# A gather of 32,768 expert rows: two tables with one indirect DMA each, against one table with the up row beside the down row

## The reference

```
query = (ht @ w_query).reshape(t, 8, 2, 128)
sub_scores = einsum('thpd,hpkd->thpk', query, sub_keys)
half_vals, half_idx = top_k(sub_scores, 16)
...                                          # 16 x 16 candidates, top 16 of them
experts = i1 * 128 + i2
gates = softmax(top_vals)
u = expert_down[experts]
act = gelu(einsum('td,thkd->thk', x, u)) * gates
vv = expert_up[experts]
out = einsum('thk,thkd->td', act, vv)
```

## Time and profile before

| what | value |
|---|---|
| time, median of 3 runs | 1837.53 us (1836.64 to 1842.37) |
| span of the profiled execution, first to last instruction | 1792.6 us |
| median less span | 44.9 us |
| first gather issued, last gather issued | 342.6 us, 1051.2 us |
| first matmul of the stage after the gathers | 1074.4 us |
| busy: PE, DVE, POOL, ACT | 78%, 59%, 39%, 26% of the span |
| bytes by the gathers | 268.47 MB |

### The profile page before, as it was taken

How to read it: one execution, slowest core, us unless ns; L and a number is a source line. 1 busy time by engine, 2 the same in 40 slices (tenths; PEclk the granted TensorE clock), 3 DMA queues, 4 the chain that set the end, 5 groups by cost and what they waited for, 6 DMA issues and landing times.

```text
span 1792.6 us, 16903 instructions
## 1 busy us (share of the span) xinstructions
PE 1399.6 (78%) x6336; PEld 971.5 (54%) x6336; DVE 1062.6 (59%) x1736; ACT 469.3 (26%) x708; POOL 694.8 (39%) x643
## 2 busy tenths in 40 slices
PE   1698858756766767787777779856999979879997
PEld 1696547722322222232222238745999877669996
DVE  3546854999987744644444435466544557664545
ACT  0332343211111111211111123232443335324331
POOL 1205600277878777777777730000111105102110
PEclk9999978978999999899999999967999989989999
DMA  8744552599999999999999963204455524335550
GB/s 261 257 162 150 205 164 95 202 348 358 358 336 348 362 379 403 405 387 409 410 407 407 410 248 138 98 1 164 157 198 188 188 97 141 109 132 182 189 188 24
DMA packets 160066, 433.17 MB, mean 242 GB/s; under 512 B 17120, under 2 KB 17376, under 8 KB 159856
## 3 DMA queue, kind: packets, MB, share of 16 engines
q0 software_dynamic: 73728, 268.47, 39.0%
q1 hardware_dynamic: 79344, 159.89, 25.6%
q10 hardware_dynamic: 6912, 3.73, 0.8%
HBM read 431.00 MB, written 1.05 MB: 241 GB/s over the span
## 4 chain that ended last, share of the span: by engine, by line
PE 42%; DVE 24%; POOL 14%; DMA 8%; issue 6%; ACT 4%; ACTq 1%; DVEq 0%
PE PS L43 41%; POOL PR L37 7%; POOL SCR L37 6%; DMA SCR<-in_expert_up,EI 5%; DVE PR L76 4%; DMA PR<-in_expert_down,EI 3%; DVE WL L73 2%; DVE LNV L61 2%; DVE LNV L49 2%; DVE GV L73 2%; ACT WH L22 2%; PE PS L82 2%; DVE X L61 2%; DVE LNV L46 1%; ACTq L34 1%
## 5 line engine op out<-in xcount | busy, mean ns | idle before, releaser
L43 PE MATMUL PS<-SCR,BIG 128*128 128x512 f32 x1024 | 507.9, 632 | 188.0 <-DMA SCR<-in_expert_up,EI 98.3
L43 PEld LDWEIGHTS PS<-SCR,BIG 128*128 128x128 f32 x1024 | 187.6, 198 | 507.1 <-issue 371.7
L76 DVE CUSTOM_DVE_ANT_0 PR<-PR,Y 128x1024 f32<-128x1024 f32 x256 | 312.3, 1222 | 223.5 <-DMA PR<-in_expert_down,EI 223.2
L73 DVE TENSOR_TENSOR WL<-W,WH 128x4096 fp32r<-128x4096 f32 x60 | 266.4, 4440 | 211.3 <-ACT WH L22 210.4
L37 POOL DMA_INDIRECT PR<-in_expert_down,EI x256 | 268.3, 1048 | 197.6 <-DVE ST L58 115.2
L37 POOL DMA_INDIRECT SCR<-in_expert_up,EI x256 | 278.5, 1088 | 80.4 <-issue 60.4
L43 PE MATMUL PS<-XH,WH 128*128 128x256 f32 x960 | 277.2, 289 | 15.1 <-POOL XL L73 9.5
L43 PE MATMUL PS<-XH,WL 128*128 128x256 f32 x960 | 272.8, 284 | 0.0
L43 PE MATMUL PS<-XL,WH 128*128 128x256 f32 x960 | 272.7, 284 | 0.0
L22 ACT ACTIVATE WH<-W 128x4096 fp32r<-128x4096 f32 x60 | 217.6, 3626 | 117.5 <-PE PS L43 104.3
L73 POOL TENSOR_TENSOR AL<-Y,AH 128x512 fp32r<-128x512 f32 x32 | 41.8, 1307 | 489.2 <-DVE AH L64 489.2
(11 more groups left out here) (166 smaller groups left out, 1467.3 us busy)
## 6 DMA issues: line engine op xcount, KB each, us to landing
W<-in_ffn_w SPq DMA_DIRECT2D x32, 2048.0 KB, 8.8
W<-in_w_ada SPq DMA_DIRECT2D x12, 2048.0 KB, 8.3
W<-in_w_in SPq DMA_DIRECT2D x6, 2048.0 KB, 7.9
W<-in_hy_w_in SPq DMA_DIRECT2D x6, 2048.0 KB, 8.1
W<-in_gla_w_in SPq DMA_DIRECT2D x6, 2048.0 KB, 7.8
W<-in_w_query SPq DMA_DIRECT2D x4, 2048.0 KB, 8.2
W<-in_w_out SPq DMA_DIRECT2D x2, 2048.0 KB, 8.4
PR<-in_expert_down,EI POOLq DMA_INDIRECT x256, 6.6
```

What stands on the lines that cost most here:

```text
L43: return lambda e: e.matmul(*a, **k)
L73: return lambda e: e.tensor_tensor(*a, **k)
L76: return lambda e: e.tensor_tensor_reduce(*a, **k)
```

## The change

The host lays the down row and the up row of an expert side by side in one table `experts` of 2048 columns. One indirect DMA fetches both for a slot, 8 KB for each partition, into one of 8 buffers `EBUF` that together take the place of `PR0` and `SCR`. The dot reads the first half, the matmuls the second. A buffer is free after the matmuls. Gates are computed for 2 slots at a time, `up` follows two slots behind the dot where it was 12, the steps of `later` come three after each dot from the first slot on, and the first split after the gathers is recorded behind the loop, with the subtraction on POOL in place of DVE.

```diff
-        PR0 = sb("PR0", [128, 8192])
-        SCR = sb("SCR", [128, 8192])
+        EB = sb("EB", [128, 16384])
+        SCR = EB[:, 8192:16384]
...
-        def split(later=False):
+        def split(later=False, by=dve):
...
-                td = dve(lambda e: e.tensor_tensor(WL[p][:, :, :], W[:, s, :, :], WH[p][:, :, :].bitcast(F32), ALU.subtract),
-                         ta, tw, *free)
+                td = by(lambda e: e.tensor_tensor(WL[p][:, :, :], W[:, s, :, :], WH[p][:, :, :].bitcast(F32), ALU.subtract),
+                        ta, tw, *free)
...
+        EBUF = [EB[:, i * 2048:(i + 1) * 2048] for i in range(NB)]
+        es = [Slot(sem(f"s_e{i}")) for i in range(NB)]
+        e_free = [pair_free[i // 4] for i in range(NB)]
...
-        LAG, GRP, EARLY = 12, 8, 8
+        GRP, LAG = 2, 3
...
+        def gather(s):
             t, j = s // 128, s % 128
+            i = s % NB
+            landed[s] = pool.dma(lambda e: e.indirect_dma_start(
+                out=EBUF[i], out_offset=None, in_=A["experts"][:, :],
+                in_offset=bass.IndirectOffsetOnAxis(ap=EI[:, t, j:j + 1], axis=0)), es[i], *e_free[i], t_e[t, j // 32])
+
+        def dot(s):
+            u = EBUF[s % NB][:, 0:1024]
+            return dve(lambda e: e.tensor_tensor_reduce(
+                out=u, in0=u, in1=Y[:, s // 128, :], scale=1.0, scalar=0.0,
+                op0=ALU.mult, op1=ALU.add, accum_out=dots[:, s:s + 1]), landed[s], ordered=False)
...
-            up_tok[s] = gather(UB[i], A["expert_up"], s, us[i], u_free[i])
...
-            pe.wait(tg, up_tok[s], *bank_free[4 + 2 * t], *bank_free[5 + 2 * t])
-            u = UB[s % NB]
+            pe.wait(tg, landed[s], *bank_free[4 + 2 * t], *bank_free[5 + 2 * t])
+            u = EBUF[s % NB]
...
-            u_free[s % NB] = (tk,)
+            e_free[s % NB] = (tk,)
...
-        for s in range(EARLY, total + LAG + 1):
+        for s in range(total + LAG):
             if s < total:
-                down(s)
-                for _ in range((4 if s < 40 else 3) if s < 112 else len(later)):
+                gather(s)
+                td = dot(s)
+                if s % GRP == GRP - 1:
+                    ta = gelu(s, td)
+                for _ in range(3 if s < 112 else len(later)):
...
-            while nu < total and nu <= s - LAG and nu in gated and n < 2:
+            while nu < total and nu <= s - LAG + 1 and nu in gated:
...
+                if nu == total - 4:
+                    pair_free[0] = (tk,)
         assert nu == total
+        split(by=pool)
         t_xt = (t_xt0, finish(1, tk))
...
+    give("experts", np.concatenate([inputs["expert_down"][0], inputs["expert_up"][0]], axis=1))
```

More of the change, by code:

```diff
@@ L1118, in build, with gelu, gate @@
         dg_free = [q_free[1] for _ in range(NDG)]
-        LAG, GRP, EARLY = 12, 8, 8
+        GRP, LAG = 2, 3
         total = 256
-        up_tok = {}
-        gated = {}
-        def gather(dst, table, s, slot, free):
+        landed, gated = {}, {}
+        def gather(s):
             t, j = s // 128, s % 128
[L1126 to L1130, removed]
             i = s % NB
[L1132 to L1138, removed]
+            landed[s] = pool.dma(lambda e: e.indirect_dma_start(
[6 more added lines that the diff above has]
+                op0=ALU.mult, op1=ALU.add, accum_out=dots[:, s:s + 1]), landed[s], ordered=False)
+        def gelu(s, td):
             g = slice(s - GRP + 1, s + 1)
-            ta = act(lambda e: e.activation(acts[:, g], dots[:, g], ACT.Gelu), dve.last)
+            return act(lambda e: e.activation(acts[:, g], dots[:, g], ACT.Gelu), td)
+        def gate(s, ta):
+            g = slice(s - GRP + 1, s + 1)
             td = dve(lambda e: e.tensor_tensor(
@@ L1148, in up @@
             t, j = s // 128, s % 128
-            i = s % NB
-            up_tok[s] = gather(UB[i], A["expert_up"], s, us[i], u_free[i])
             i = s % NDG
             tg = act(lambda e: e.activation(DG[i], ident, ACT.Copy, scale=acts[:, s:s + 1]), *dg_free[i], gated[s], ordered=False)
-            pe.wait(tg, up_tok[s], *bank_free[4 + 2 * t], *bank_free[5 + 2 * t])
-            u = UB[s % NB]
+            pe.wait(tg, landed[s], *bank_free[4 + 2 * t], *bank_free[5 + 2 * t])
+            u = EBUF[s % NB]
             for n in range(2):
-                make = lambda e: e.matmul(PS[4 + 2 * t + n][:, :], DG[i], u[:, n * 512:(n + 1) * 512],
+                make = lambda e: e.matmul(PS[4 + 2 * t + n][:, :], DG[i], u[:, 1024 + n * 512:1536 + n * 512],
                                           start=(j == 0), stop=(j == 127))
@@ L1186, in finish @@
             return turn_tile(X[:, t, :], t, tx)
-        for s in range(EARLY):
-            down(s)
-            later.pop(0)()
-        for s in range(GRP - 1, EARLY, GRP):
-            gate(s)
         nu = 0
-        for s in range(EARLY, total + LAG + 1):
+        for s in range(total + LAG):
             if s < total:
-                down(s)
-                for _ in range((4 if s < 40 else 3) if s < 112 else len(later)):
+                gather(s)
[3 more added lines that the diff above has]
+                for _ in range(3 if s < 112 else len(later)):
                     if later:
@@ L1208, in build @@
                 if s % GRP == GRP - 1:
[L1209 to L1213, removed]
-            while nu < total and nu <= s - LAG and nu in gated and n < 2:
+                    gate(s, ta)
+            while nu < total and nu <= s - LAG + 1 and nu in gated:
                 tk = up(nu)
                 nu += 1
-                n += 1
                 if nu == 128:
                     t_xt0 = finish(0, tk)
+                if nu == total - 4:
+                    pair_free[0] = (tk,)
         assert nu == total
+        split(by=pool)
         t_xt = (t_xt0, finish(1, tk))
@@ L1638 @@
 _LAYERED = ["w_ada", "b_ada", "g_norm_mix", "w_in", "b_forget", "g_out_fox", "g_out_sb", "w_out", "g_norm_ffn",
-            "w_query", "sub_keys", "expert_down", "expert_up", "hy_w_in_2", "diff_lambda_2", "diff_subln_2",
+            "w_query", "sub_keys", "hy_w_in_2", "diff_lambda_2", "diff_subln_2",
             "hy_w_out_2", "gla_w_in_2", "gla_w_gate_up_2", "gla_b_gate_2", "gla_norm_2", "gla_w_out_2"]
```

## The result

| | before | after |
|---|---|---|
| time, median | 1837.09 us (1836.36 to 1842.37, 4 runs) | 1760.49 us (1758.87 to 1761.89, 4 runs) |
| span of the profiled execution | 1792.6 us | 1758.7 us |
| first matmul of the stage after the gathers | 1074.43 us | 1040.73 us |

The ratio is 0.958 (95% interval 0.956 to 0.960): the change takes 76.6 us off. The forecast was 1788 us with a range of 1766 to 1816, so the sign was right and the size too small by 28 us. Set against the profiled execution of before, the stage that the change touches gained only 33.7 us (1074.43 to 1040.73). The two differences don't fit together, and that is the main question of the experiments.

What follows compares the result with a forecast made beforehand. Two nearly equal limits, POOL's issue and the DMA engines, with DVE right behind POOL in the earlier part. Next stage at 998 + 26.2 = 1024.6, 49.8 us less; span 1792.6 - 49.8 = 1742.8, plus 44.9: 1788 us, range 1766 to 1816.

Steps and rivals of the forecast that it cites:

- plus the 44.9 around it: Last term: time outside the profiled span, median of the runs less the span, added to 1742.8 us to give 1788.
- The sum inside the span: Next stage after the gathers starts at 1024.6 instead of 1074.4 us, 49.8 less, so span 1792.6 becomes 1742.8.
- The rival of 2.56: Gathers: an 8 KB row costs two of 4 KB, slot stays at 2.56 us, 11 us later: 1799; chance 0.20.
- Dot 98: Earlier part of the gathers: DVE sets the pace, 2.57 us for each slot, and this dot ends at 606 us.
- The rival that this part stays at 361 GB/s: Earlier part of the gathers: something other than POOL's issue holds the engines, 2.9 us a slot: 1824 us; chance 0.10.
- the slower rival: Gathers: eight buffers are too few, 2.74 us for each slot, next stage 8 us later: 1845 us; chance 0.08.
- The later part: Gathers from 606 us: 154 slots at 2.49 us, plus 4 for constants and 5 for `finish(0)`; last slot lands at 998.
- T + 26.2: Start of the next stage, counted from T, the last slot's landing at 998 us; includes `finish(1)` waiting for POOL's subtraction.
- The rival without this wait: End of the gathers: `finish(1)` does not wait on POOL, next stage at T + 17.9, time 1780 us; chance 0.15.

Runs made afterwards that it cites:

- the second profile of before: The kernel before, unchanged, profiled and timed again: 1837.6 us, ratio 0.998; span of the profiled run 1832.6 us.
- the run with the slower pace: After, with three and two steps of the choice in turn behind the dots instead of three, constants at slot 120 instead of 112: 1751.28 us, ratio 0.951.

## Why the prediction was wrong, point by point

**The step that failed: "plus the 44.9 around it".** I took the median less the span as a constant that any execution carries. It is 1.8 or 1.9 us in every run that has both. The rest of the 44.9 was time inside the gathers that usual executions of before lose and the profiled one did not. After doesn't lose it, so I carried 43 us into the forecast that were not there. The sum inside the span erred by 16 us the other way, and the two leave the 28. That they cancel in part is luck: with 1.8 in place of 44.9 the same sum gives 1745 us, 16 too few. (998 + 26.2 is 1024.2; the 1024.6 of the sum comes of unrounded terms.)

**What the 44.9 us were.** The earlier trace rows said that POOL's 512 gathers fill the later part with nothing to spare, and I read that as a limit equal to the transfer's. The 18 us of waiting that I read there were mostly the ordinary pause of 0.30; only three waits were longer, 5.6 us in all. An engine without reserve has a second price: each wait is lost for good. In the second profile of before, 37 of the 47 us that the gathers take longer are such waits. The Trainium skill (Perfetto Trace Analysis, "What "DMA-bound" means") names the issuing engine's sequencer as a bound of its own beside the DMA engines, and large descriptors as what matters for both. The runs agree: a gather of 128 rows took POOL the same 0.94 us with rows of 32 bytes, 4 KB and 8 KB, so rows of twice the length halve POOL's work for the same bytes. Whether POOL's time goes by DMAs or by rows is not separated, since every gather here has 128 rows. The runs with memsets show both prices with all DMAs as in after: 2.48 us of POOL for a slot cost 23 us, 2.87 us cost 74. What starts the long waits in usual executions of before stays open. They are 2 to 7 us each where PE frees the buffer and up to 4.8 us where the profile says "remote". The stops of DVE that come with them occur only in profiles with 512 gathers, also where half of them fetch 32 bytes, and not where memsets fill POOL instead; so POOL's lack of reserve explains that the time was lost, and not that the engines stopped. Why the first profiled execution had none of these stops stays open too.

**The transfer.** I took 2.49 us for a slot between 2.36 and 2.56; it is 2.49 (421 GB/s). The rival of 2.56 fell. In the trace's packets a row of 8 KB is one packet and takes 309 to 312 ns at the median; a row of 4 KB took 159 before, so two take 318. At eight rows for each of the 16 engines, 9 ns less for a row is an estimated 0.07 us of a slot, which is the step that I took. The times don't show it by themselves: before, POOL's own 2.56 hid what 4 KB rows can do.

**DVE in the first slots.** Dot 98, the 99th, was forecast to end at 606 us. It ended at 613.75:

```profile
361.93 0.16 DVE L73 TENSOR_TENSOR BIG<-BIG,LNV 128x2 f32<-128x2 f32 x1 [4.08 <-ACT BIG L22]
...
612.53 1.22 DVE L76 CUSTOM_DVE_ANT_0 EB<-EB,Y 128x1024 f32<-128x1024 f32 x1
```

DVE set the pace, with 0.5 us of wait for rows, and the run with the slower pace shows it; so the mechanism was right and the sum 8 us short. Half of that is the first gate, which waited 4.08 us for a GELU that stood on ACT behind other work and a table load, a wait that the sum left out. From there the pace was 2.60 us for a slot ((608.96 - 362.01) / 95), not 2.57. The rival that this part stays at 361 GB/s fell with 421; the share of 0.97 on which it stood is no sign of a limit.

**Buffers.** Landing took 10.8 us and POOL always waited for a buffer, yet DMA stood at 421 GB/s. Eight are enough while nothing interrupts; the slower rival fell.

**The later part, 18 us too short.** I put the last landing at 998 us; it came at 1016.4. From 606 on, the stretches give 366 x 44 + 420 x 50 + 354 x 50 + 421 x 266 = 166.8 MB, less 1.8 of constants, which is 157 slots. I had 154. At 606 us 99 slots had landed and 96 dots were done, where I had 102 and 99: three slots did lie ahead of DVE, but DVE was three slots late. That is 8 us. `finish(0)` lost (421 - 354) / 421 x 50 = 8 us where I took 5 of a range from 2.67 to 10.1. And 606 to 650 us lost 55 / 421 x 44 = 6 us, which I had at nothing: the softmax's Exp in `later` makes ACT load its tables twice, GELU and diagonals stand behind that, and POOL waits 5.51 us at 616.5:

```profile
610.50 1.28 ACT L22 ACT_TABLE_LOAD   x1
...
612.45 8.91 PE L43 MATMUL PS<-EB,BIG 128*128 128x512 f32 x13 [3.70 <-ACT BIG L22]
...
613.19 1.28 ACT L22 ACT_TABLE_LOAD   x1
...
616.50 1.35 POOL L37 DMA_INDIRECT EB<-in_experts,EI  x1 [5.51 <-PE PS L43]
```

The table load is only the start of it. After its 3.70 us of idleness PE ran at the lower of its two clock levels, a granted 0.50, for some 6 us, with 8 matmuls in 6.2 us, where it then did 26 in 11.4 (columns as in the earlier trace rows):

```profile
612.40:618.60 6.20, 6.16 (x8) 2.54 (x9) 5.55 (x15) 2.96 (x7) 1.35 (x1) 0.50 0.61 218
618.60:630.00 11.40, 10.91 (x26) 4.58 (x24) 4.73 (x9) 1.41 (x5) 6.96 (x7) 1.00 0.95 349
```

How much of the 6 us is the idleness and how much the slower matmuls is not separated. Two to three slots between dot and up don't cover this. The constants (1.8 MB) cost 4 us as put.

**The end.** T + 26.2 was forecast, T + 24.3 measured (1016.4 to 1040.73). The wait of `X<-X,Y` for POOL was put at 8 us and cost 7.63 against 0.69. The Trainium skill (SBUF — State Buffer, "Who interferes with whom") has it as a VectorE instruction with two SBUF inputs and a GpSimd one that reads SBUF excluding each other; the trace agrees, and with the subtraction on DVE `X<-X,Y` took 0.69 us again, 3.6 us less up to the next stage. The rival without this wait fell.

## What to carry to other kernels

Compare the span of a profile with the times before using either: where they differ by more than the few us that surround a span, the profile is of an unusual execution, and the terms of a sum must be scaled to the usual one. An engine whose instructions stand back to back is worth more to relieve than the difference to the next limit, since each wait is lost for good there. And when a pipeline's lag is cut, go through everything that stops one of its engines for a few us (table loads, a closing step, a large load): what lies in front of it is then on the path.

## What the runs showed of the hardware

An indirect DMA of 128 rows took POOL 0.93 to 0.94 us at best whether a row had 32 bytes, 4 KB or 8 KB, plus a pause of 0.30 us behind another gather, or 0.15 behind a memset.

DMA's busy share is no measure of its limit here: it stood at 0.97 for 361 GB/s and 1.02 for 407 in the earlier trace rows, at 1.01 for 421 in after, and the same packets counted 57 us longer when they were issued late.

At the median a packet of the trace took 84 ns for 2 KB, 159 for 4 KB and 309 to 312 for 8 KB on its DMA engine.

With 512 gathers, three of four profiles show DVE standing still for 0.5 to 3.4 us before instructions that wait only for DVE's own; none of the eight profiles with 256 gathers does.
